# Two transformer blocks on one core: expert output scattered by pairs, no meeting before the second block, first gather between weight chunks, output in token order

## The reference, cut to what matters

```
x = [1, 512, 1024]; ctx = [1, 256, 1024]
for l in 0, 1:                                   # first block, two layers
    h  = modulate(rmsnorm(x, g_mix), shift, scale)
    p  = h @ w_in                                # q, k, v of two branches, conv, gates
    x += gt1 * (gated sum of attention A, attention B, short conv) @ w_out
    h2 = modulate(rmsnorm(x, g_ffn), shift, scale)
    aff = softmax(h2 @ w_router); gate, idx = top 64 tokens of each of 16 experts
    y_e = (silu(h2[idx] @ w_g[e]) * (h2[idx] @ w_u[e])) @ w_d[e]      # 16 experts
    x[idx] += gt2 * gate * y_e
    # layer 0 does the same for ctx (32 tokens of each expert)
hdn = rmsnorm(x, norm_gain)                      # second block
q_a, k_a, v_a, g_a, q_b, k_b, v_b, g_b = hdn @ w_in_2
q, k = rope(rmsnorm(q)), rope(rmsnorm(k))        # heads of 64
o_a = banded attention(A) * silu(g_a);  o_b = dilated attention(B) * silu(g_b)
out = x + concat(o_a, o_b) @ w_out_2
```

## Time and profile before

| | |
|---|---|
| median of 3 runs | 3319.41 us (3317.58 to 3319.48) |
| the profiled execution | 3320.36 us, of which the span of its instructions is 3318.6 us |
| PE busy | 3154.6 us (95%) |
| DVE, ACT busy | 1078.3 us, 628.6 us |
| HBM read | 547.63 MB |
| granted TensorE clock, mean | 0.985 |

### The profile page before, as it was taken

One profiled execution on the slowest core, in us unless ns is written; L12 is line 12 of the kernel. 1 busy time (PEld: TensorE's weight loads), 2 busy tenths in 40 slices (PEclk: granted clock), 3 DMA queues, 4 the chain that ended last, 5 costly groups with the idle time before them and its releaser, 6 DMA issues. The chain is left out here.

```text
span 3318.6 us, 34530 instructions
## 1 busy us (share of the span) xinstructions
PE 3154.6 (95%) x13661; PEld 1539.9 (46%) x13661; DVE 1078.3 (32%) x1552; ACT 628.6 (19%) x1109; POOL 16.7 (1%) x35
## 2 busy tenths in 40 slices
PE   7999999999997999999989999999979999989998
PEld 4665555555553333333334655444433333234544
DVE  5654544455532111111117554011120110127351
ACT  3145520000011111111112354000111001021151
POOL 1000000000000000000000000000000000000000
PEclk9999999999998999999999999999989999999999
DMA  7020023435314878787870200222259999962200
GB/s 232 1 77 26 1 77 120 163 111 170 133 64 155 307 278 307 278 306 278 323 204 0 77 20 20 76 76 89 76 204 409 409 409 409 409 205 64 64 1 26
DMA packets 299298, 551.98 MB, mean 166 GB/s; under 512 B 62744, under 2 KB 137768, under 8 KB 299016
## 3 DMA queue, kind: packets, MB, share of 16 engines
q1 hardware_dynamic: 297232, 546.53, 46.0%
q0 software_dynamic: 1600, 3.20, 0.3%
q10 hardware_dynamic: 312, 0.05, 0.0%
HBM read 547.63 MB, written 2.10 MB: 166 GB/s over the span
## 5 line engine op out<-in xcount | busy, mean ns | idle before, releaser
L822 PE MATMUL ps<-hT,ring 128*128 128x512 f32 (+1 forms) x2128 | 797.1, 532 | 16.1 <-ACT hT L1407 16.1
L822 PEld LDWEIGHTS ps<-hT,ring 128*128 128x128 f32 x2128 | 405.7, 191 | 394.2 <-issue 372.6
L1250 PE MATMUL ps<-ring,hT 128*64 128x512 f32 x1536 | 354.8, 600 | 31.0 <-DMA ring<-in_w_e_down 16.8
L1114 PE MATMUL ps<-ring,hT 128*64 128x512 f32 x1536 | 350.8, 598 | 1.5 <-ACT hT L1407 1.5
L1250 PEld LDWEIGHTS ps<-ring,hT 128*64 128x64 f32 x1536 | 100.4, 136 | 259.1 <-issue 187.8
L1114 PEld LDWEIGHTS ps<-ring,hT 128*64 128x64 f32 x1536 | 101.7, 136 | 235.6 <-issue 235.2
L822 PE MATMUL ps<-obuf,ring 128*128 128x512 f32 (+1 forms) x512 | 198.3, 540 | 0.9 <-issue 0.9
L838 PE MATMUL ps<-hT,ring 128*128 128x512 f32 (+1 forms) x448 | 191.3, 555 | 0.3 <-DVEq L1392 0.2
L1120 PE MATMUL ps<-ring,hT 128*32 128x512 f32 x1536 | 184.7, 598 | 0.0
L1407 ACT ACTIVATE prob<-ps 128x512 f32<-128x512 f32 (+1 forms) x68 | 47.0, 692 | 683.7 <-PE ps L822 683.7
L1407 ACT ACTIVATE prob<-prob,nms 128x768 f32<-128x768 f32 (+5 forms) x224 | 159.1, 710 | 21.0 <-DVE nms L1961 13.9
(11 more groups left out here) (259 smaller groups left out, 2768.3 us busy)
## 6 DMA issues: line engine op xcount, KB each, us to landing
ring<-in_w_e_gate SPq DMA_DIRECT2D x128, 512.0 KB, 6.8
ring<-in_w_e_up SPq DMA_DIRECT2D x128, 512.0 KB, 6.7
ring<-in_w_e_down SPq DMA_DIRECT2D x128, 512.0 KB, 6.5
ring<-in_w_e_gate SPq DMA_DIRECT2D x64, 1024.0 KB, 11.9
ring<-in_w_e_up SPq DMA_DIRECT2D x64, 1024.0 KB, 11.7
ring<-in_w_e_down SPq DMA_DIRECT2D x64, 1024.0 KB, 10.6
ring<-in_w_in SPq DMA_DIRECT2D x49, 1024.0 KB, 5.3
ring<-in_w_ada SPq DMA_DIRECT2D x48, 1024.0 KB, 6.2
```

Source lines behind the costliest of these rows:

```text
L822: mm = pe.matmul(ps[:, b + a:b + e], lhs[:, k, :], rhs[:, k, a:e], start=k == 0, stop=k == nk - 1)
L1114: mm = pe.matmul(ps[e * CX:(e + 1) * CX, b + pair * 512:b + (pair + 1) * 512], lhs[:, k, s0:s0 + CX], expert_dst(0, slot, e)[:, k % 2, :], ...
L1250: mm = pe.matmul(ps[e * CX:(e + 1) * CX, b + h * 512:b + (h + 1) * 512], lhs[:, k, s0:s0 + CX], expert_dst(1, slot, 0)[:, e, h * 512:(h + ...
```

## The change

1. **Scatter by pairs.** The last round's `out` pieces become 16: eight for the first pair of experts, which stand between the last six chunks and just behind them, and eight for the second pair behind all chunks. DVE adds each to `xT`.
2. **No meeting behind them; three projections on unscaled input.** `into_second`: as soon as a piece d of `xT` is complete, ACT writes it times the gain to `m3` and its square to `h3`. PE (`first_raw`) accumulates the projection `ka` and the sum of squares, piece by piece, between the last scatter pieces. `ka`, `qa0` and `qa1` (RAW) are products of `m3`; DVE multiplies their results by the inverse root, and then makes `h3` from `m3`. POOL loads the tables earlier, behind layer 1's last attention output.
3. **First gather between chunks, more places.** Each of the first eight chunks follows the gather piece it needs. The chunks of layer 1's experts from the seventh on go round nine places instead of six (three new ones in `obuf`, `vbuf` and `merged`), filled as soon as these buffers are free.
4. **Token-order ending.** Eight jobs `xt` of four transposes each turn `xT` into token order during attention of the second block (side jobs of steps 16 to 23; PSUM bank SIDE, copied by ACT). The output product has the tokens as its rows: 16 jobs `wt` of 16 instructions of 256 columns; DVE adds each to the turned x, and SP stores 16 pieces of 128 KB. The meeting, the last transposes, ACT's copies and POOL's stores are gone.
5. **Order in all three attentions.** The side job of a step now stands behind Q and the first T, not ahead of them.

```
-                if side:
-                    order += side.pop(0)
                 if s % 4 == 0 and 4 <= s <= n:
                     order.append(("Q", l, s // 4 - 1))
                 if banks:
                     order.append(("T", l, s - 1, 0))
+                if side:
+                    order += side.pop(0)
...
+            if i + 1 == ROUNDS:
+                for d in range(6):
+                    at[42 + d] = [("out", i, d, 0)]
...
-        PAIR_STEPS += [("piece", ("out", ROUNDS - 1, d)) for d in range(KD)]
+        PAIR_STEPS += [("piece", ("out", ROUNDS - 1, d, 0)) for d in (6, 7)]
+        PAIR_STEPS += [("piece", ("out", ROUNDS - 1, d, 1)) for d in range(KD)]
...
+            if key[0:2] == ("expert", 1) and r >= RING:
+                s = r if r < RING + MORE else chunk_at[n - RING - MORE][0]
...
+            def into_second():
+                A.need(amp_ready, (2, 0))
+                for d in range(KD):
+                    A.need(pair_added, ("out", ROUNDS - 1, d, 1))
+                    A.do(func(m3[:, d, 0:NX], xT[:, d, 0:NX], ACT.Identity, bias=zero3[:, d, 0:1], scale=amp4[:, 2, 0, d, 0:1]),
+                         hpre, (2, "mix", d, 0))
+                    A.do(func(h3[:, d, 0:NX], xT[:, d, 0:NX], ACT.Square), sq_ready, ("n", 2, "mix", d))
+                root(rsn, ("norm", 2, "mix"), NX, D)
...
+                        if step[1][0:2] == ("out", ROUNDS - 1) and step[1][3] and step[1][2] >= 3:
+                            first_raw(step[1][2] - 3)
...
+                if (i, w, pair) == (0, "eg", 0):
+                    need(pair_in, ("in", 0, k))
...
+                    if j in RAW:
+                        V.do(v.tensor_tensor(qk_dest(*j[1:])[:, 0:w], ps[:, b:b + w], rsn, ALU.mult), raw_scaled, j)
...
+                    if j == RAW[0]:
+                        for d in range(KD):
+                            V.do(v.tensor_tensor(h3[:, d, 0:NX], m3[:, d, 0:NX], rsn, ALU.mult), h_ready, (2, "mix", d, 0))
...
+                elif kind == "wt":
+                    b = V.read(j)
+                    V.do(v.tensor_tensor(xtok[t][:, m, :], xtok[t][:, m, :], ps[:, b:b + CH], ALU.add), out_added, j)
...
+            for j in of("wt"):
+                sp.wait_ge(out_added.sem, out_added.at[j])
+                sp.dma_start(out[0, t * P:(t + 1) * P, m * CH:(m + 1) * CH], xtok[t][:, m, :]).then_inc(s_out, 16)
```

More of the change, by code:

```diff
@@ L215, in program @@
         s_param = [s_param, sem("param_loaded1")]
[L216 removed]
+        w_full = [sem(f"weights_landed{i}") for i in range(RING + MORE)]
         full = [sem(f"psum_full{i}") for i in range(5)]
@@ L278, in side_steps @@
                     steps[-1].append(("silg", l, d))
-                return steps
+                return steps + [[("xt", l, t, h)] for t in range(NX // P) for h in range(2)]
             for m in range(4):
@@ L493, in program @@
         PAIR_STEPS = []
-        PAIR_STEPS += [("piece", ("in", 0, d)) for d in range(KD)]
         for i in range(ROUNDS):
             pieces_at = side_pieces(i)
+            if i == 0:
+                pieces_at.update({d: [("in", 0, d)] for d in range(KD)})
             for r in range(len(WEIGHT_ORDER) * KD):
@@ L818, in product @@
                     for k in range(nk):
-                        if ph is not None and (ph, k, a) not in seen_h:
+                        if key in RAW:
+                            rhs = m3
+                        elif ph is not None and (ph, k, a) not in seen_h:
                             need(h_ready, ph + (k, a))
@@ L842, in run @@
                         chunk_end[cn] = (full[SIDE], job[key][2])
+                elif kind == "xt":
+                    t, h = j[2:]
+                    b = begin(j, SIDE)
+                    for n in range(4):
+                        mm = pe.transpose(ps[:, b + n * P:b + (n + 1) * P], xT[:, 4 * h + n, t * P:(t + 1) * P], ident)
+                    part(mm, j)
+                elif kind == "wt":
+                    m, t = j[2:]
+                    if m == 0 and t == 0:
+                        need(oT_ready, ("O", 2, 2 * TILES[2] - 1))
+                    cn, slot = weights(chunk_of(j)[0])
+                    b = begin(j)
+                    for k in range(KD):
+                        mm = pe.matmul(ps[:, b:b + CH], o2[:, k, t * P:(t + 1) * P], ring3(slot)[:, k, :],
+                                       start=k == 0, stop=k == KD - 1)
+                    part(mm, j)
+                    chunk_end[cn] = (full[job[j][0]], job[j][2])
                 elif kind in ("conv_c", "conv_x") or kind == "silg" and j in job:
@@ L1233, in bank_clear, with first_raw @@
                         need(pair_copied, ("ht", i, pair))
+                def first_raw(d):
+                    if d == 0:
+                        begin(RAW[0])
+                        begin(("norm", 2, "mix"))
+                    cn, slot = weights(chunk_of(RAW[0])[0])
+                    need(hpre, (2, "mix", d, 0))
+                    b = BANK[job[RAW[0]][0]]
+                    mm = pe.matmul(ps[:, b:b + NX], ring3(slot)[:, d, 0:P], m3[:, d, 0:NX], start=d == 0, stop=d == KD - 1)
+                    if d == KD - 1:
+                        part(mm, RAW[0])
+                        chunk_end[cn] = (full[job[RAW[0]][0]], job[RAW[0]][2])
+                    b = BANK[job["norm", 2, "mix"][0]]
+                    need(sq_ready, ("n", 2, "mix", d))
+                    mm = pe.matmul(ps[:, b:b + NX], ones[:, :], h3[:, d, 0:NX], start=d == 0, stop=d == KD - 1)
+                    if d == KD - 1:
+                        part(mm, ("norm", 2, "mix"))
                 for step in PAIR_STEPS:
@@ L1254, in experts_second @@
                     chunk_end[n] = (pair_used.sem, pair_used.at[step[1:]])
-                meet()
+                for d in range(KD - 3, KD):
+                    first_raw(d)
             pe.wait_ge(s_ident, 16)
@@ L1277, in _ @@
                 (experts_first, experts_second)[l]()
-            norm_sum((2, "mix"), NX)
-            for j in PLAN[2]:
+            for j in PLAN[2][1:]:
                 run(j)
-            meet()
-            for t in range(NX // P):
-                b = begin(("out", t))
-                for k in range(KD):
-                    mm = pe.transpose(ps[:, b + k * P:b + (k + 1) * P], xT[:, k, t * P:(t + 1) * P], ident)
-                part(mm, ("out", t))
         @block.sync
@@ L1704, in _ @@
                 (experts_first, experts_second)[l]()
-            norm((2, "mix"), NX)
+            into_second()
             for j in PLAN[2]:
                 run(j)
-            A.meet()
-            for t in range(NX // P):
-                b = A.read(("out", t))
-                A.do(sc.copy(tok[:, t, :], ps[:, b:b + D]), out_copied, t)
-                A.release(("out", t))
         @block.vector
```

136 lines of the change are left out of this document (79 added, 57 removed).

## The result

| | before | after |
|---|---|---|
| median | 3318.65 us (3317.58 to 3319.48, 4 runs) | 3285.10 us (3282.93 to 3285.59, 4 runs) |
| profiled execution | 3320.36 us, span 3318.6 | 3282.93 us, span 3281.1 |

(The median of three runs given ahead of the prediction was 3319.41; a fourth run moved it by 0.8 us.) The ratio is 0.9897 (95% interval 0.9885 to 0.9910): 33.5 us faster, where 21.6 were forecast, and 0.9 us outside the range. The sign and the large terms were right, the size was not.

The account below looks back on a forecast made before the run. Bounds: PE in projections, weights' arrival narrowly in experts, latency chains at the seam and in late attention, a tail at the end. Terms -21.3 + 4 - 2 + 5.2 - 7.5 = -21.6 gave 3297.8 us by the median; range 3286 to 3309.

Parts of the forecast that it names:

- C: Order and xt jobs in the attentions: -2 us in layers 0 and 1, +9.2 in the second block.
- D: End of the kernel, behind the last product: 6.5 us instead of 14.0, so -7.5, bounds -5.5 and -9.
- a term of -2: Layers 0 and 1: the new order changes time by between -5.5 and +4 us, taken as -2.
- one of +4 for the tanhs: Second block's attention: tanh now ahead of the exponentials on ACT, +1.0 us in each of four steps, +4.
- the 3.4 us behind the last landing: End of the kernel: 3.4 us from the last store's landing to the span's end, taken as unchanged.
- A: Start of layer 1's experts: the weight stream restarts later but ten chunks further on, -4.1 us, net 2.6 at the last chunk.
- B: Seam from last chunk to second block: scatter by pairs and early projections; with the experts' start -21.3 us, stage alone -18.7.
- the 2.6 us allowed for low clock: Experts' start: one chunk more and one gather at half speed cost some 2.6 us more, an estimate.
- R3: Rival: clock stays low through the experts' first eight steps: 3321 us (chance 0.04), or slower if it lasts longer (0.04).
- The xt copies: Second block's attention: eight ACT copies join the loop T, copy, exponentials, T: +0.65 us each, +5.2.
- R1: Rival: attention's additions are hidden, clock rises, so +4 and +5.2 go: 3288.6 us, chance 0.15.
- the bound of -9: End of the kernel: the largest gain allowed for the new ending, -9 us, against -7.5 forecast.

Follow-up runs that it names:

- e4: Kernel before with its four last stores issued by SP instead of POOL: 3314.31 us, 0.9986 of before.
- e7: Kernel after with six places instead of nine in layer 1's experts, first gather still between chunks: 3293.26 us, 0.9922 of before.
- e11: Kernel after with the new order only in the row-sum steps of layers 0 and 1, the old order everywhere else: 3283.66 us, 0.9898 of before.
- e1: Kernel before with the new order alone (side job behind the first T in all three attentions): 3311.75 us, 0.9978 of before.
- e8: Kernel after with the eight xt copies on DVE instead of ACT: 3282.06 us, 0.9891 of before.
- e3: Kernel after with the old order in the second block's attention, the new one kept in layers 0 and 1: 3280.46 us, 0.9881 of before.
- e5: Kernel after with its 16 last stores issued by POOL instead of SP: 3290.18 us, 0.9915 of before.

## Why the prediction was wrong where it was

The steps that failed are in C and D: the price of the new order in the three attentions (a term of -2 where -7.6 came, and one of +4 for the tanhs, which cost 1.2), and the 3.4 us behind the last landing, which D kept and which went with POOL's queue.

**A and B held.** The start of the experts was forecast as one sum of steps, stop, landing and stream and came to -2.7 for -2.6 at the last chunk; the seam came to -19.1 for -18.7. Each step is in the profile: chunk 0 at 4.57 behind the gather (4.45), the pitch 4.67 (4.5), `qa0` 24.9 behind the last chunk (25.8). That the sums agree so closely is luck: chunk 16 landed 1.3 us sooner than forecast, since the 2.6 us allowed for low clock did not come in this execution, and from there to the last chunk it took 453.0 us for 451.7; sister kernels with the same code here stand at 497.5 to 499.9, and B of before is 212.3, but 210.9 in e4. But A was right as a sum of two things of opposite sign that it did not price apart: "nine places cover that, six would not" is what e7 shows, yet that the interleaving itself was a loss beside nine places was not said. The rival R3, low clock through the eight steps, did not come: the pitch was that of full clock from the second gather on. The stops of 0.81 by themselves did not bring the clock down, nor did the 0.9 in after's attention. The Trainium skill, TensorE: Matmul & The Clock Gate, section "A second HAM failure mode: psum-queue depth-cycling", names short idles as a cause of swings. Before's late steps at 0.61 and e4's at 0.88 agree with it; after's at 1.00, with stops as long, do not.

**C, layers 0 and 1: -2 for -7.6, the largest miss.** The step that failed is the choice between -5.5 and +4. The +4 was half of 14 ACT copies ahead of the exponentials, a cost taken over from the second block; in after, TensorE waits for ACT's exponentials 0.5 us in all of layer 0's attention and not at all in layer 1's, so those copies are hidden. And the good end was not the end: R's row of 5.5 us gives the idle time, while the V to V pitch of such a step falls by 0.6 to 0.7 for a wait of 0.37 to 0.49, as the overlap of two runs is lost at a stop too. The falls are there in e11 step by step (8.2 us in 13 steps); longer waits for VectorE's copies, which the prediction did not have, take part of them back.

**C, second block: +9.2 for +4.1.** The tanh's chain was right, its price was not: the four steps grew by 0.34, 0.77, 0.77 and 0.26, and after the small gain of the plain steps V stands 1.6 us later, not 4. The forecast took four equal steps of 4.6 us from T to T; it was 4.4 in two of them, and less in the first (3.96 from V to V, before 3.62) and the last (3.12, before 2.86). In e1, without xt jobs, the last fell by 0.18 instead, so the tanhs alone cost 1.2; why the first and the last cost less was not taken apart. The xt copies were forecast at +5.2; with the new order they cost 5.8, by the mechanism named (e8, e3). The order without xt jobs came to 107.3 in e1, 1.7 less than before and the same as e4, which has before's code there and a spell shorter by 10.3 us: -1.7 + 5.8 = 4.1. So R1's number was nearer than the forecast, but its reason, hidden copies, fell; the clock did stay up.

**D: -7.5 for -11.3.** The step that failed took the 3.4 us behind the last landing over from the old ending (3.0 by its own rows). That went with POOL's queue, and with SP's it was 0.4: e4 and e5 give 3.9 and 4.0 us for the queue in all. The landing, put at 2.5, took 1.8. With 1.8 and the 3.4 kept the sum is 5.7 behind the product, or -8.3, inside the bound of -9; what broke the bound is the 3.4 alone.

**The whole.** C's two halves and D, and 1.2 us ahead of layer 0 that no part of the change explains (188.2 to 190.5 in all kernels), make up 16 us between the two profiled spans, of which 12.7 remain between the medians. All four misses had the same sign. The low end of the range, 3286, stood 2.6 us under R1, the only rival that was faster than the forecast, and no rival let D gain more.

## What to carry to other kernels

Where one engine closes a loop (TensorE's transposes, ACT's copy and exponentials, TensorE again), a copy is nearly free ahead of the transposes (0.4 us for eight) and costs its full length behind them; two edits that are each nearly free, an order and a job, can cost 5.8 us together, so price them together. A wait of R for a copy is removed by giving the copy's source first and a long product second. Price buffers and interleaving apart: more places let the stream start at the first use, and interleaving delays exactly that use. And let the hardware queue issue a kernel's last stores.

## What the runs showed of the hardware

- The end of the span comes 0.4 us behind the last landing with stores from SP (after, e4, e8), and 3.0 (before, e1) and 4.0 (e5) with stores from POOL; in all SP instead of POOL is worth 3.9 and 4.0 us once per launch, in two kernels.
- The clock's low spells are not a fixed cost of a piece of code: the same steps ran at 0.61 and at 0.88 in two kernels (109.0 and 107.3 us for the stage), and the clock rose 4.4 us behind the gather's start in after and 8.2 to 9.2 behind it in six kernels with the same instructions there, so that the first chunk took 1.94 us in one and 3.68 in e7.
- Steps with TensorE busy 9.58 of 14 us and stops of 0.9 in each ran at a granted clock of 1.00 in after, and eight steps with stops of 0.81 ran at 1.00 at the start of its experts. Before's seam, in which TensorE stopped for 7.33 us ahead of `ka`, had 0.50 for 6.8 us there; after's seam, without a stop over 0.2, had 1.00 throughout.
- Stops of 0.37 to 0.49 us cost 0.6 to 0.7 of a step, as two runs of TensorE that follow each other overlap by 0.16 in the rows.
